# Narrower GpSimd pieces, another group order and fewer row transfers in a bidirectional mLSTM and attention encoder layer

## The chip, the cores and the metric

The kernel runs on one core of one Trainium2 chip. A core has a matrix engine (TensorE, PE in the profile, with PEld for its weight loads), a vector engine (VectorE, DVE), a scalar engine (ScalarE, ACT), GpSimd (POOL), a queue engine (SyncE, SP) that here only issues transfers, 16 DMA engines, the on-chip memory SBUF and the accumulator memory PSUM with 8 banks of 2 KB a partition. The metric is device time in microseconds of one execution, the median of several.

## What is computed

One encoder layer is applied with the same parameters to two sequences, of 256 and 1024 tokens (T = 1280 columns, NB = 10 blocks of 128), model width 1024. Cut to what matters here:

```python
h = rmsnorm(x, pre_mix_norm)
z = h @ w_in + b_in                       # all projections, float32 accuracy
ya = windowed_gqa_attention(aq, ak, av)   # 16 heads in 4 groups, window 128
ym = bidirectional_mlstm(mq, mk, mv, mo, mi, mf)   # 4 heads, both directions
merged = g_att * (ya @ w_att_branch) + g_mlstm * (ym @ w_mlstm_branch)
x = x + rmsnorm(merged @ w_out, post_mix_norm)
# then a gated FFN with a depthwise convolution, and a residual

# one chunk of 128 tokens of the mLSTM, one direction, one head (width 256)
a = (q @ k.T) * exp(d - m_t)              # masked decay weights
num = w_inter * (q @ C) + a @ v           # state product, values product
den = w_inter * (q @ n) + sum(a)
h = num / max(abs(den), exp(-m_t))
C_new = decay * C + wk.T @ v              # state, carried to the next chunk
```

## The kernel before, in words

**Units and groups.** Every weight matrix lies in HBM as units of 1024 x 128. A unit is loaded to `unit_raw` and split by GpSimd in `take` into a high part `unit_h` (a multiplication by one, rounded, line 701) and a low part `unit_l` (the rest, line 704). TensorE multiplies high by high, high by low and low by high, 8 inner tiles each, so one group (`unit_group`, lines 1762 to 1764) is 24 matmuls of 512 or, in each third group of a unit, 256 columns. For each of the 4 heads there are 22 groups M (mLSTM queries, keys, values and output gate; 12 and up run as `vo_group`, lines 1795 to 1797) and 21 groups A (gates, attention queries, keys, values). A group goes to PSUM bank 0 or 1; `group_tables` sets which, by the group's number modulo 2, and `bank_free` lets the group wait until the last user of its bank is copied out. There are five unit slots, so a load waits for the last group of the unit five before it.

**A head.** `mlstm(h)` runs 10 steps i. In step i the forward direction does chunk i and the backward one chunk 9 - i. On TensorE a step is: `m_numden` (state product of both directions, line 1856, and values product, line 1859, in banks 3 and 4), the forward state update (`m_update`, line 1873), the first A group that the table `A_STEP` names for the step, the backward update, scores and turned keys of the next step while i < 4 (`m_scores`, lines 1841 and 1843), and the other A groups of the step. A direction has no state product in its first chunk of a sequence. After the steps come the groups A18 to A20, then the first M group of the next head, and then `attend(h)`: ten blocks j, each with turned probabilities (line 1960), scores of the next block (line 1941), two M groups of the next head (`M_BESIDE`) and the values product (lines 1973 and 1974). The last head has no M groups to put beside its attention. After the four heads follow the branch, output and FFN products, which split their weights in another function, `split`.

**The other engines in a step.** VectorE, in its written order: `normalise_h(i)` (lines 1381 to 1396), forward `state` (line 1370 or 1372, c_st), `weights(i+1)` (line 1361, ex times the kept scores), from step 5 on `gated(i)` (lines 1407 and 1410), `gate_ahead(i+1)` (a reciprocal, line 1399), and then backward `state`. ScalarE makes the exponents `ex` from rows in `bw` (line 1049), copies scores and keys out of PSUM (`keep_scores`, lines 1056 and 1057), copies the groups out (line 978), and issues `load_rows` (line 1013), two transfers a step, one for each direction. GpSimd masks the rows (line 721), scales queries and keys (lines 730 and 745) and, after some steps (`A_TAKE`), takes a unit.

**Between heads.** `c_st`, the state, lies where `ya_st`, the attention's output, was staged. Before, VectorE ends `attend` with a wait for the transfers of `ya_st` to HBM (s_ya) and TensorE ends it with a wait for the last addition (a_o). The first thing that VectorE does in a head is to copy the head's columns (lines 1416 to 1421), for which ScalarE waits (m_sel) before its first exponents. The rows of steps 0 and 1 of the next head are loaded in attention block 9.

## Time and profile before

| | us |
|---|---|
| median of 3 runs (2757.56 to 2759.15) | 2758.14 |
| the profiled execution | 2762.94 |
| its span in the trace | 2761.1 |
| TensorE busy in it (92% of the span) | 2547.2 |
| VectorE busy | 1506.0 |
| GpSimd busy | 1170.9 |
| ScalarE busy | 665.6 |
| mean granted TensorE clock, as a share of full | 0.962 |

The profiled execution is 4.8 us above the median, and 1.8 us of it lie around the span. A busy share is an average over the whole program. The four heads take about the time from 170 to 1500 us of the trace; head 1 starts at 488, head 2 at 816, head 3 at 1143. TensorE's idle time is in few places, and each has a releaser, the instruction of another engine whose end let it go on.

### The profile page before, as it was taken

What the parts mean: (1) busy time and instruction counts of PE and PEld (TensorE: products, weight loads), DVE (VectorE), ACT (ScalarE), POOL (GpSimd) and SP (SyncE); (2) the same over time, 40 slices, a digit from 0 to 9 for tenths busy, and PEclk for the clock granted to TensorE, in tenths of its full rate; (3) what the DMA queues carried; (4) which work ended last, traced back from release to release, by engine and by line L of the source; (5) the groups of instructions that cost most, each with busy time, mean ns of one, the idle gap of its engine ahead of it and who ended that gap; (6) DMA issues with size and microseconds to landing.
All of it is one profiled execution on the core that took longest, in us unless ns stands there. A gap on an engine that the chain in (4) does not pass through costs nothing.

```text
span 2761.1 us, 37750 instructions
## 1 busy us (share of the span) xinstructions
PE 2547.2 (92%) x14636; PEld 2325.3 (84%) x14636; DVE 1506.0 (55%) x2133; ACT 665.6 (24%) x1511; POOL 1170.9 (42%) x658
## 2 busy tenths in 40 slices
PE   7999899898989899898688999897999999999996
PEld 4888778787878788786577899897999999999996
DVE  5524467154652647435674655888874217876312
ACT  4112333133422333223433112321110101110001
POOL 5434320342104421142412236565566656666663
PEclk9999999999999999999799999999999999999998
DMA  3122111331122211223234342323323343232321
GB/s 128 43 81 86 58 31 28 88 92 35 37 63 66 77 40 33 69 77 122 90 115 134 111 154 69 138 70 102 102 70 119 103 139 97 76 114 70 115 82 61
DMA packets 128583, 233.77 MB, mean 85 GB/s; under 512 B 11000, under 2 KB 73992, under 8 KB 128448
## 3 DMA queue, kind: packets, MB, share of 16 engines
q1 hardware_dynamic: 77920, 203.04, 22.6%
q10 hardware_dynamic: 50528, 28.89, 4.4%
q8 instruction: 89, 1.46, 0.2%
q14 instruction: 46, 0.38, 0.0%
HBM read 184.35 MB, written 47.46 MB: 84 GB/s over the span
## 4 chain that ended last, share of the span: by engine, by line
PE 79%; DVE 13%; ACT 3%; DMA 2%; DVEq 2%; issue 1%; SPq 0%; ACTq 0%
PE ps L1762 20%; PE ps L1764 20%; PE ps L1763 20%; PE ps L1795 2%; PE ps L1797 2%; PE ps L1941 2%; PE ps L1796 2%; PE ps L1960 2%; PE ps L1856 2%; PE ps L1873 2%; DVE prob L1470 2%; PE ps L1859 1%; DMA ya_scratch<-ya_st 1%; DVE acc L1605 1%; ACT prob L1143 1%
## 5 line engine op out<-in xcount | busy, mean ns | idle before, releaser
L690 POOL TENSOR_TENSOR ring_h<-raw,colt 128x1024 fp32r<-128x1024 f32 x168 | 326.7, 1945 | 649.4 <-PE ps L1764 645.0
L1762 PE MATMUL ps<-h_h,ring_h 128*128 128x320 f32 (+1 forms) x1408 | 439.9, 312 | 14.7 <-DVE f_z L1669 9.1
L1763 PE MATMUL ps<-h_l,ring_h 128*128 128x320 f32 (+1 forms) x1408 | 438.6, 312 | 0.0
L1764 PE MATMUL ps<-h_h,ring_l 128*128 128x320 f32 (+1 forms) x1408 | 438.5, 311 | 0.0
L693 POOL TENSOR_TENSOR ring_l<-raw,ring_h 128x1024 fp32r<-128x1024 f32 x168 | 415.8, 2475 | 23.9
L1762 PE MATMUL ps<-ht_h,unit_h 128*128 128x512 f32 (+1 forms) x1080 | 396.4, 367 | 5.9 <-ACT av_t L978 4.8
L1763 PE MATMUL ps<-ht_l,unit_h 128*128 128x512 f32 (+1 forms) x1080 | 383.9, 356 | 0.0
L1764 PE MATMUL ps<-ht_h,unit_l 128*128 128x512 f32 (+1 forms) x1080 | 383.9, 355 | 0.0
L1605 DVE TENSOR_TENSOR acc<-acc,sq 128x322 f32<-128x322 f32 (+1 forms) x84 | 114.9, 1368 | 311.9 <-ACT sq L816 310.1
L1762 PEld LDWEIGHTS ps<-h_h,ring_h 128*128 128x128 f32 x1408 | 267.3, 190 | 16.1 <-issue 9.8
L1764 PEld LDWEIGHTS ps<-h_h,ring_l 128*128 128x128 f32 x1408 | 267.6, 190 | 0.0
L1763 PEld LDWEIGHTS ps<-h_l,ring_h 128*128 128x128 f32 x1408 | 267.2, 190 | 0.4 <-issue 0.2
L701 POOL TENSOR_TENSOR unit_h<-unit_raw,colt 128x1024 fp32r<-128x1024 f32 x61 | 118.7, 1946 | 299.2 <-DMA unit_raw<-w 299.2
L1762 PEld LDWEIGHTS ps<-ht_h,unit_h 128*128 128x128 f32 x1080 | 205.7, 190 | 35.0 <-issue 6.4
L1764 PEld LDWEIGHTS ps<-ht_h,unit_l 128*128 128x128 f32 x1080 | 204.7, 190 | 29.4
L1763 PEld LDWEIGHTS ps<-ht_l,unit_h 128*128 128x128 f32 x1080 | 205.5, 190 | 27.9 <-issue 0.2
L721 POOL TENSOR_TENSOR bw<-bw,mask 128x256 f32<-128x256 f32 x40 | 29.3, 731 | 351.6 <-DMA bw<-rows_scratch 351.6
L1762 PE MATMUL ps<-ht_h,ring_h 128*128 128x512 f32 (+3 forms) x384 | 141.5, 368 | 19.0 <-DVE ht_l L1545 9.2
L704 POOL TENSOR_TENSOR unit_l<-unit_raw,unit_h 128x1024 fp32r<-128x1024 f32 x61 | 150.7, 2471 | 8.7
L1763 PE MATMUL ps<-ht_l,ring_h 128*128 128x512 f32 (+3 forms) x384 | 138.8, 362 | 0.0
L1764 PE MATMUL ps<-ht_h,ring_l 128*128 128x512 f32 (+3 forms) x384 | 138.6, 361 | 0.0
L1763 PE MATMUL ps<-f_z,ring_h 128*128 128x320 f32 x448 | 138.4, 309 | 0.0
(244 smaller groups left out, 5293.4 us busy)
## 6 DMA issues: line engine op xcount, KB each, us to landing
raw<-w SPq DMA_DIRECT2D x168, 512.0 KB, 3.6
unit_raw<-w SPq DMA_DIRECT2D x61, 512.0 KB, 3.9
bw<-rows_scratch ACTq DMA_DIRECT2D x80, 128.0 KB, 4.8
gate_scratch<-g_st SPq DMA_DIRECT2D x32, 256.0 KB, 3.9
xr<-xt SPq DMA_DIRECT2D x2, 2568.0 KB, 10.0
x_scratch<-x SPq DMA_DIRECT2D x2, 2568.0 KB, 8.9
zo_scratch<-o_st SPq DMA_DIRECT2D x40, 128.0 KB, 1.7
ym_scratch<-y_st ACTq DMA_DIRECT2D x40, 128.0 KB, 2.0
```

What stands on the lines that cost most here:

```text
L690: nc.gpsimd.tensor_tensor(ring_h[:, :, slot * P:(slot + 1) * P], raw[:, rslot], one_col.unsqueeze(2).to_broadcast([P, KT, P]), ALU.mult)
L693: nc.gpsimd.tensor_tensor(ring_l[:, :, slot * P:(slot + 1) * P], raw[:, rslot], ring_h[:, :, slot * P:(slot + 1) * P].bitcast(F32), ALU.su ...
L701: nc.gpsimd.tensor_tensor(unit_h[:, slot], unit_raw[:, slot], one_col.unsqueeze(2).to_broadcast([P, KT, P]), ALU.mult)
L704: nc.gpsimd.tensor_tensor(unit_l[:, slot], unit_raw[:, slot], unit_h[:, slot].bitcast(F32), ALU.subtract).then_inc(s_split, 1)
L1470: last = V.tensor_scalar(prob[:, r, a:b], prob[:, r, a:b], small[:, 36 + r:37 + r], None, ALU.mult)
L1605: V.tensor_tensor(acc[st][:, a:b], acc[st][:, a:b], sq[st][:, j % slots, 0:b - a], ALU.add)
L1762: mm(out_ap, wh, hi(k + k_first), start=first and k == 0, stop=False)
L1763: mm(out_ap, wh, lo(k + k_first), start=False, stop=False)
L1764: ins = mm(out_ap, wl, hi(k + k_first), start=False, stop=last and k == kts - 1)
L1795: mm(ps[:, g % 2, :], ht_h[:, k, t], unit_h[:, 0:4, k], start=k == 0, stop=False)
L1796: mm(ps[:, g % 2, :], ht_h[:, k, t], unit_l[:, 0:4, k], start=False, stop=False)
L1797: ins = mm(ps[:, g % 2, :], ht_l[:, k, t], unit_h[:, 0:4, k], start=False, stop=k == KT - 1)
```

## The change

Six edits. (1) `take` splits a unit in four pieces of two inner tiles (256 columns) for each of its two operations; `split` is left as it is. (2) In `m_numden` the values product is put in front of the state product; its wait (m_a) is now in front of those for the scaled queries (m_q) and the state (m_c). (3) Two A groups instead of one run ahead of step 0, and `A_STEP` shifts: step 0 has [2], step 3 only [7], step 8 has [16, 17], step 9 [18], and A19 and A20 come after; ScalarE's exponents of step 1 come ahead of the steps. (4) `load_rows` is one transfer a step for both directions, from a new scratch tensor in which the two rows of a chunk lie side by side (1 KB in a piece instead of 512 bytes); those of the next head are issued in attention block 8 instead of 9. (5) Banks alternate by a group's place in the whole order instead of its number. (6) For all but the last head, VectorE's wait for s_ya and TensorE's wait for a_o move from the end of `attend` into step 0 of the next head, to where the state and its bank are first written; for the last head VectorE's is left out, TensorE's stays.

The diff, its core:

```diff
-A_STEP = [[1]] + [[2 * i, 2 * i + 1] for i in range(1, 8)] + [[16], [17]]
+A_STEP = [[2], [3, 4], [5, 6], [7], [8, 9], [10, 11], [12, 13], [14, 15], [16, 17], [18]]
...
-        bank = key[2] % 2
+        bank = i % 2
...
+            for d in range(2):
+                sp.dma_start(uw_d.rearrange("(r c) q t -> r q c t", c=NB)[4 * d:4 * d + 4, 0],
+                             r_u[32 * d:32 * d + 4, :].rearrange("p (c t) -> p c t", t=P)).then_inc(p_out, 16)
...
-                nc.gpsimd.tensor_tensor(unit_h[:, slot], unit_raw[:, slot],
-                                        one_col.unsqueeze(2).to_broadcast([P, KT, P]), ALU.mult)
+                for k in range(0, KT, 2):
+                    nc.gpsimd.tensor_tensor(unit_h[:, slot, k:k + 2], unit_raw[:, slot, k:k + 2],
+                                            one_col.unsqueeze(2).to_broadcast([P, 2, P]), ALU.mult)
                 pool.drain()
-                nc.gpsimd.tensor_tensor(unit_l[:, slot], unit_raw[:, slot], unit_h[:, slot].bitcast(F32),
-                                        ALU.subtract).then_inc(s_split, 1)
+                for k in range(0, KT, 2):
+                    last = nc.gpsimd.tensor_tensor(unit_l[:, slot, k:k + 2], unit_raw[:, slot, k:k + 2],
+                                                   unit_h[:, slot, k:k + 2].bitcast(F32), ALU.subtract)
+                last.then_inc(s_split, 1)
...
-                pool.wait_ge(m_bw[i % 2], lin(lambda k: 32 * (5 * k + i // 2 + 1), h))
+                pool.wait_ge(m_bw[i % 2], lin(lambda k: 16 * (5 * k + i // 2 + 1), h))
...
-                for d in range(2):
-                    c = chunk_of(d, i)
-                    act.dma_start(bw[:, i % 2, d], rows_d[0:2, bass.ds(h + (4 * d + shift), 1), c * P:(c + 1) * P]
-                                  .rearrange("q o t -> o q t").to_broadcast([P, 2, P])).then_inc(m_bw[i % 2], 16)
+                a, b = [(4 * d + h + shift) * NB + chunk_of(d, i) for d in range(2)]
+                act.dma_start(bw[:, i % 2].rearrange("p d q t -> p d (q t)"),
+                              uw_d.rearrange("(o n) q t -> o n (q t)", o=1)[:, a:b + 1:b - a]
+                              .to_broadcast([P, 2, 2 * P])).then_inc(m_bw[i % 2], 16)
...
                 evac_a(0, h)
+                exponents(1, h)
+                evac_a(1, h)
                 for i in range(NB):
-                    if i + 1 < NB:
+                    if 1 <= i < NB - 1:
                         exponents(i + 1, h)
...
+                    if dense and j == NB - 2:
+                        act.wait_ge(a_s_done, lin(lambda k: NB * (k + 1), h))
+                        for i in range(2):
+                            load_rows(i, h, 1)
...
-                    if dense and j == NB - 1:
-                        act.wait_ge(a_s_done, lin(lambda k: NB * (k + 1), h))
-                        for i in range(2):
-                            load_rows(i, h, 1)
...
                 dve.wait_ge(m_cu[d], lin(lambda k: 8 * k + updates_to(d, i), h))
+                if i == 0 and h:
+                    dve.wait_ge(s_ya, 16 * NB * h)
...
-                dve.wait_ge(s_ya, lin(lambda k: 16 * NB * (k + 1), h))
...
                 else:
+                    pe.wait_ge(m_h, lin(lambda k: NB * k + i, h))
+                pe.wait_ge(m_a, lin(lambda k: NB * k + i + 1, h))
+                for d in range(2):
+                    ins = mm(ps[:, 3 + d, 0:DH + 1], ex[i % 2][:, side(d, i)], v_tok[:, chunk_of(d, i)],
+                             start=True, stop=fresh(d, i))
+                if i:
                     pe.wait_ge(m_q, lin(lambda k: 9 * k + i, h))
-                    pe.wait_ge(m_h, lin(lambda k: NB * k + i, h))
                 for d in range(2):
                     if not fresh(d, i):
                         pe.wait_ge(m_c[d], lin(lambda k: 8 * k + updates_to(d, i - 1), h))
                         for dt in range(2):
-                            mm(ps[:, 3 + d, 0:DH + 1], qw[:, d, dt], c_st[:, d, dt], start=dt == 0, stop=False)
-                pe.wait_ge(m_a, lin(lambda k: NB * k + i + 1, h))
-                for d in range(2):
-                    ins = mm(ps[:, 3 + d, 0:DH + 1], ex[i % 2][:, side(d, i)], v_tok[:, chunk_of(d, i)],
-                             start=fresh(d, i), stop=True)
+                            ins = mm(ps[:, 3 + d, 0:DH + 1], qw[:, d, dt], c_st[:, d, dt], start=False, stop=dt == 1)
                 ins.then_inc(m_nd, 1)
...
                 pe.wait_ge(m_wk, lin(lambda k: 9 * k + i + 1, h))
+                if i == 0 and d == 0 and h:
+                    pe.wait_ge(a_o, NB * h)
...
                 m_scores(0, h)
-                unit_group("A", 0, 0, h)
+                for g in range(2):
+                    unit_group("A", 0, g, h)
...
-                for g in range(18, 21):
+                for g in range(19, 21):
                     unit_group("A", g // 3, g % 3, h)
...
-                pe.wait_ge(a_o, lin(lambda k: NB * (k + 1), h))
+                    pe.wait_ge(a_o, NB * HEADS)
```

VectorE at the seam of heads 0 and 1, from the last addition of the attention to the first weights of the mLSTM. Before:

```order
L1517 TENSOR_TENSOR ya_st<-ya_st,ps 64x512 [waits a_out_lo_part]
L1416 COPY hc<-tokcol 128x10 [waits m_y_evacuated,ya_stored]
...
L1476 COPY hc<-colt 128x2
L1361 TENSOR_TENSOR ex_79<-ex_79,s_sv 128x256 [waits m_exp,m_scores_and_keys_kept]
L1381 SCALAR_TENSOR_TENSOR small<-ps,hc 128x2 [waits m_numden]
```

After:

```order
L1528 TENSOR_TENSOR ya_st<-ya_st,ps 64x512 [waits a_out_lo_part]
L1427 COPY hc<-tokcol 128x10 [waits m_y_evacuated]
...
L1487 COPY hc<-colt 128x2
L1370 TENSOR_TENSOR ex_79<-ex_79,s_sv 128x256 [waits m_exp,m_scores_and_keys_kept]
L1392 SCALAR_TENSOR_TENSOR small<-ps,hc 128x2 [waits m_numden]
...
L1381 COPY c_st<-ps 128x514 [waits ya_stored,m_update_fwd]
```

The wait for the stored attention output has moved from the copy of the columns to the first write of the state, which comes after the normalisation of step 0.

ScalarE at the same seam (bw are the rows, ex the exponents, s_sv and mk_t the kept scores and keys, g_st a group's copy). Before:

```order
L1151 ACTIVATE prob_h<-ps 128x512 x2
L1180 DMA ya_scratch<-ya_st 64x4x128
L1013 DMA bw<-rows_scratch 128x2x128 x4
L1175 ACTIVATE ya_st<-ps 64x512
L1180 DMA ya_scratch<-ya_st 64x4x128
L1049 ACTIVATE ex_79<-bw,tokcol 128x128 x2
L1056 ACTIVATE s_sv<-ps 128x256
L1057 ACTIVATE mk_t<-ps 128x2x2x128
L978 ACTIVATE g_st<-ps,hc 128x512
```

After:

```order
L1019 DMA bw<-exponent_rows_scratch 128x2x256 x2
L1184 ACTIVATE ya_st<-ps 64x512
L1160 ACTIVATE prob_h<-ps 128x512 x2
L1189 DMA ya_scratch<-ya_st 64x4x128
L1184 ACTIVATE ya_st<-ps 64x512
L1189 DMA ya_scratch<-ya_st 64x4x128
L1056 ACTIVATE ex_79<-bw,tokcol 128x128 x2
L1063 ACTIVATE s_sv<-ps 128x256
L1064 ACTIVATE mk_t<-ps 128x2x2x128
L985 ACTIVATE g_st<-ps,hc 128x512
```

Four row transfers in block 9 have become two in block 8, one block of the attention earlier.

TensorE at the end of step 0 of head 0 and the start of step 1 (a row of x2 stands for one direction's or both directions' matmuls). Before:

```order
L1873 MATMUL ps<-v_tok,wk 128x257 x2
L1841 MATMUL ps<-ident,mk_t 128x128 x2
L1843 MATMUL ps<-mq_t,mk_t 128x128 x2
L1841 MATMUL ps<-ident,mk_t 128x128 x2
L1843 MATMUL ps<-mq_t,mk_t 128x128 x2
L1856 MATMUL ps<-c_st,qw 128x257 x4
L1859 MATMUL ps<-v_tok,ex_80 128x257 x2
L1762 MATMUL ps<-ht_h,unit_h 128x256
```

After:

```order
L1852 MATMUL ps<-ident,mk_t 128x128 x2
L1854 MATMUL ps<-mq_t,mk_t 128x128 x2
L1852 MATMUL ps<-ident,mk_t 128x128 x2
L1854 MATMUL ps<-mq_t,mk_t 128x128 x2
L1864 MATMUL ps<-v_tok,ex_80 128x257 x2
L1872 MATMUL ps<-c_st,qw 128x257 x4
L1771 MATMUL ps<-ht_h,unit_h 128x512
```

Directly behind the scores stands now the values product, which needs the weights ex made from these scores. In step 4 the same rows follow one another after the change; before, the group A7 stood between the scores and step 4.

## Rows read from the trace of the kernel before

**Rows 1.** TensorE's waits from 187 to 1290: total us, times, longest.

```profile
PE ps L1856 <- DVE c_st L1370: 29.0, 7, 8.2
PE ps L1859 <- DVE ex L1361: 20.7, 3, 7.5
PE ps L1960 <- DVE prob L1470: 20.6, 9, 3.4
PE ps L1762 <- ACT av_t L978: 4.8, 3, 1.6
```

**Rows 2.** Timeline, seam of heads 0 and 1: start us, us, row, [idle before <-releaser].

```profile
487.30 4.51 SPq L481 DMA_DIRECT2D unit_raw<-w  x4
...
488.44 0.44 PE L1841 MATMUL ps<-ident,mk_t 128*128 128x128 f32 x2 [1.40 <-DVE ya_st L1517]
...
500.05 0.17 DVE L1416 COPY hc<-tokcol 128x10 f32<-128x10 f32 x1 [11.66 <-DMA ya_scratch<-ya_st]
...
502.95 2.05 PE L1859 MATMUL ps<-v_tok,ex 128*128 128x257 f32 x4 [7.49 <-DVE ex L1361]
```

**Rows 3.** Windows: us; busy PE, PEld, DVE, ACT, POOL; granted clock; DMA share, GB/s.

```profile
502.90:507.40 4.50, 4.45 (x11) 3.54 (x12) 2.00 (x6) 0.60 (x3) 4.36 (x4) 0.50 0.15 58
303.00:306.00 3.00, 3.00 (x7) 2.44 (x8) 0.00 (x0) 0.00 (x0) 0.00 (x0) 0.50 0.00 0
350.60:353.80 3.20, 3.14 (x15) 3.14 (x16) 0.00 (x1) 1.09 (x2) 0.00 (x0) 0.50 0.00 0
392.30:398.10 5.80, 5.72 (x25) 5.63 (x26) 0.62 (x2) 0.00 (x0) 0.00 (x0) 0.50 0.00 0
325.20:328.20 3.00, 3.00 (x13) 2.51 (x14) 0.00 (x0) 0.00 (x0) 0.96 (x1) 1.00 0.35 130
```

**Rows 4.** Timeline of head 0, steps 8 and 9.

```profile
286.40 0.16 DVE L1381 SCALAR_TENSOR_TENSOR small<-ps,hc 128x2 f32<-128x2 f32 x1 [3.56 <-PE ps L1859]
...
290.12 4.48 DVE L1407 TENSOR_TENSOR h_acc<-h_acc,o_ld_even 128x256 f32<-128x256 f32 x2
...
292.24 2.08 POOL L701 TENSOR_TENSOR unit_h<-unit_raw,colt 128x1024 fp32r<-128x1024 f32 x1
...
294.68 2.40 DVE L1410 SCALAR_TENSOR_TENSOR o_ld_even<-h_acc 128x256 f32<-128x256 f32 x1
...
302.99 2.08 PE L1856 MATMUL ps<-c_st,qw 128*128 128x257 f32 x4 [8.10 <-DVE c_st L1370]
```

**Rows 5.** Timelines of GpSimd and VectorE in the last head, steps 7 and 8.

```profile
1257.55 1.36 POOL L745 TENSOR_TENSOR wk<-mk_t,tokcol 128x256 f32<-128x256 f32 x2
...
1257.66 0.78 DVE L1361 TENSOR_TENSOR ex<-ex,s_sv 128x256 f32<-128x256 f32 x1
...
1269.55 0.76 DVE L1407 TENSOR_TENSOR h_acc<-h_acc,o_ld_even 128x256 f32<-128x256 f32 x2
```

**Rows 6.** GpSimd's line 745, all of it: duration ns min/median/max.

```profile
L745 POOL TENSOR_TENSOR wk<-mk_t,tokcol x64: 608/616/855, 173.8 to 1258.1; 128x256 f32<-128x256 f32 x64
```

**Rows 7.** The same for GpSimd's line 721.

```profile
L721 POOL TENSOR_TENSOR bw<-bw,mask x40: 723/732/743, 150.7 to 1265.9; 128x256 f32<-128x256 f32 x40
```

**Rows 8.** Timeline of head 0, the attention's blocks 0 and 1.

```profile
345.75 4.86 DVE L1470 TENSOR_SCALAR prob<-prob,small 128x256 f32<-128x256 f32 x4
...
350.66 1.97 PE L1960 MATMUL ps<-ident,prob 128*128 128x128 f32 x8 [3.43 <-DVE prob L1470]
...
392.38 1.97 PE L1960 MATMUL ps<-ident,prob 128*128 128x128 f32 x8 [3.11 <-DVE prob L1470]
```

**Rows 9.** Timeline of head 1, from the scores to the end of step 1's products.

```profile
514.66 1.03 PE L1856 MATMUL ps<-c_st,qw 128*128 128x257 f32 x4
...
515.76 0.43 DVE L1361 TENSOR_TENSOR ex<-ex,s_sv 128x256 f32<-128x256 f32 x1 [8.31 <-ACT mk_t L1057]
...
516.84 1.14 PE L1856 MATMUL ps<-c_st,qw 128*128 128x257 f32 x4 [1.15 <-DVE c_st L1370]
```

**Rows 10.** The page, sixth part: row transfers, KB each, us from issue to landing.

```profile
bw<-rows_scratch ACTq DMA_DIRECT2D x80, 128.0 KB, 4.8
```

More of the change, by code:

```diff
@@ L155, in build @@
     x1_d = nc.dram_tensor("x1_scratch", (2, KT, P, WIN), F32).ap()
-    rows_d = nc.dram_tensor("rows_scratch", (6, 8, T), F32).ap()
+    rows_d = nc.dram_tensor("rows_scratch", (4, 8, T), F32).ap()
+    uw_d = nc.dram_tensor("exponent_rows_scratch", (2 * HEADS * NB, 2, P), F32).ap()
     dec_d = nc.dram_tensor("decay_scratch", (8, NB), F32).ap()
@@ L531, in _ @@
             sp.wait_ge(p_args, 1)
-            for q, rows in ((0, r_u), (2, r_li), (3, r_f), (4, r_m), (5, r_b)):
+            for d in range(2):
+                sp.dma_start(uw_d.rearrange("(r c) q t -> r q c t", c=NB)[4 * d:4 * d + 4, 0],
+                             r_u[32 * d:32 * d + 4, :].rearrange("p (c t) -> p c t", t=P)).then_inc(p_out, 16)
+            for q, rows in ((0, r_li), (1, r_f), (2, r_m), (3, r_b)):
                 for d in range(2):
@@ L975, in evac @@
                 a, b = CHUNKS[key1[2] % 3]
-                src = ps[rows, key1[2] % 2, 0:b - a]
+                src = ps[rows, GROUPS[key1][1], 0:b - a]
                 act.wait_ge(d_done, lin(lambda k: GROUPS[key_of(k)][0] + 1, h))
@@ L1343, in evac_vo @@
                     dve.wait_ge(s_os[blk % 2], lin(lambda k: 16 * 5 * (k + shift), h))
-                bank = (12 + blk) % 2
+                bank = GROUPS[("M", h + shift, 12 + blk)][1]
                 V.tensor_tensor(v_tok[:, blk, 0:DH], ps[:, bank, 0:DH], bias_vo[:, 0:DH], ALU.add)
@@ L1777, in unit_group @@
                 g = 3 * u + c
+                bank = GROUPS[(kind, h + shift, g)][1]
                 unit = a_unit if kind == "A" else m_unit
@@ L1783, in unit_group @@
                 bank_free(pe, lambda k: (kind, k + shift, g), h)
-                dense(ps[:, g % 2, 0:b - a], in_unit(n1),
+                dense(ps[:, bank, 0:b - a], in_unit(n1),
                       (lambda k: ht_h[:, k, a:b], lambda k: ht_l[:, k, a:b]), before=before).then_inc(d_done, 1)
@@ L1792, in vo_group @@
                 bank_free(pe, lambda k: ("M", k + shift, g), h)
+                bank = GROUPS[("M", h + shift, g)][1]
                 t = slice(blk * P, (blk + 1) * P)
                 for k in range(KT):
-                    mm(ps[:, g % 2, :], ht_h[:, k, t], unit_h[:, 0:4, k], start=k == 0, stop=False)
-                    mm(ps[:, g % 2, :], ht_h[:, k, t], unit_l[:, 0:4, k], start=False, stop=False)
-                    ins = mm(ps[:, g % 2, :], ht_l[:, k, t], unit_h[:, 0:4, k], start=False, stop=k == KT - 1)
+                    mm(ps[:, bank, :], ht_h[:, k, t], unit_h[:, 0:4, k], start=k == 0, stop=False)
+                    mm(ps[:, bank, :], ht_h[:, k, t], unit_l[:, 0:4, k], start=False, stop=False)
+                    ins = mm(ps[:, bank, :], ht_l[:, k, t], unit_h[:, 0:4, k], start=False, stop=k == KT - 1)
                 ins.then_inc(d_done, 1)
@@ L1909, in mlstm @@
                         unit_group("A", g // 3, g % 3, h)
-                for g in range(18, 21):
+                for g in range(19, 21):
                     unit_group("A", g // 3, g % 3, h)
```

4 lines of the change are left out of this document (2 added, 2 removed).

## The prediction

> **What bounds the kernel now.** TensorE is busy for 92% of the span, so time comes or goes where it stands idle, or where it runs at half clock. I read first its list of waits from 187 to 1290 us, which is the four heads without the last attention [rows 1]: 29.0 us for the state (7 times: three of about 8.1 and four of 1.15), 20.7 for the first weights of a head (3 times), 20.6 for the normalised probabilities (6 of 3.1 to 3.4, the rest below 0.6), 4.8 for the copy of A20. Then I went to each place in the timeline. At the seam of two heads TensorE waits 1.40 us for the attention's last addition and, one group later, 7.49 us for the weights; VectorE stood 11.66 us until the attention's output had landed, and everything in the new head hangs on it [rows 2]. In step 9 of head 0 TensorE waits 8.10 us for the backward state while VectorE's operations on two SBUF operands take over 2 us each [rows 4]; in the last head, where GpSimd takes no unit there, two of them take 0.76 together and there is no such wait [rows 5]. In attention blocks 0 and 1 four multiplications of VectorE take 4.86 us beside a unit's split, and TensorE waits 3.43 and 3.11 [rows 8]. Last, the clock: behind each wait of over 3 us TensorE works at 1.2 GHz (granted 0.50) for 3.0 to 5.8 us; behind the 1.6 us wait for A20's copy it keeps 2.4 GHz (1.00) [rows 3]. A long wait therefore costs its length and about half of the slow stretch behind it.
>
> **The seams (edits 3, 4 and 6).** Removed: 20.7 us for the weights [rows 1] and 3 x 1.40 = 4.2 for the addition [rows 2], together 24.9. Behind each, 4.5 us at half clock [rows 3] cost 2.2, at three seams about 6.4. In the new order VectorE copies the columns right after the last addition at 488.4; columns, exponents, copied keys and weights took 502.8 - 500.0 = 2.8 us [rows 2], so the weights are ready at about 491.5. TensorE has the scores (488.44 to the next group, an estimate of 1.3 from 8 small products) and now two groups ahead of step 0. A matmul of 512 columns takes 3.00 / 13 = 0.23 us [rows 3], a group of 24 thus 5.5, one of 256 columns about half, 2.9. Step 0 is reached at about 487 + 1.3 + 11 = 499, with 8 us in hand. What is late next? The moved wait of VectorE stands in front of the first state, due at about 501.6 (step 0's product and the normalisation behind it); the output landed before 500.05 [rows 2], and queued behind that wait are only the weights and state of step 1, not due before 506. TensorE's moved wait is 11 us late. The row masks are made on GpSimd before the seam, as the transfers leave one block (some 9 us or more) earlier. So I take the full gain, **31.3 us**. If the output lands 3 us later nothing changes; from some 5 us on it would.
>
> **State of step 9 (edits 1, 2 and 3).** From the end of step 8's products (286.40) to the state is 302.99 - 286.40 = 16.6 us on VectorE, of which TensorE waits 8.1 and fills 8.5 [rows 4]. The new order puts group A17 (2.9) and the values product (0.9) into the stretch: 12.3 filled. VectorE's chain: two operations of line 1407 took 4.48 where 0.76 is their time [rows 4, 5], so one loses 1.9; with the two of line 1410 (2.40 for the first, which is of the same size) and the weights, 1.0, five operations lose some 8.4 us. When GpSimd works in pieces of 256 columns, an operation can lose at most one piece: 0.61 for the first kind (line 745 has that size and a multiplier that is spread the same way) [rows 6], 0.73 for the second [rows 7], so 5 x 0.65 = 3.3. The chain becomes 16.6 - 5.1 = 11.5, below 12.3: no wait. Three times 8.1 is 24.4, and 1.5 for each slow stretch [rows 3] adds 4.5: **28.9 us**. Without any help from the pieces 16.6 - 12.3 = 4.3 would stay.
>
> First what the row shows: a VectorE operation on two SBUF operands lasts 2 us beside a long GpSimd instruction, 0.4 without [rows 4, 5], and in the last head one of 0.78 got in between two GpSimd instructions of line 745, since it ended at 1258.44 and they at 1258.91 [rows 5]. The Trainium skill, SBUF — State Buffer, section Who interferes with whom, says that the pair of ports shared by the two engines is an exclusive lock, held for the whole instruction by whichever issued first. By that rule read strictly, four pieces already queued on GpSimd would be served before VectorE, and the edit would do nothing (rival 3); the last head's row speaks for taking turns.
>
> **Attention blocks 0 and 1 (edit 1).** Here four multiplications follow one another, each loses a piece: 345.75 + 4 x (0.57 + 0.27) = 349.1 instead of 350.6, if the pieces are back to back. I take 1.5 us for block 0 and 1.4 for block 1, three heads: 8.7 of 18.9. The waits that stay (1.9 and 1.7) lie between the 1.6 us behind which the clock stayed and the 3.1 behind which it fell; of the half clock's 1.6 + 2.9 = 4.5 us a head [rows 3] I take 1, so 3 in all. Together **11.7**; bounds 0 and 18.9 + 13.5 = 32.4.
>
> **Banks (edit 5).** M0 follows A20 in the other bank, the wait of 3 x 1.6 us goes [rows 1]: **4.8**. The copy of A20 is now due only in front of M0's last inner tile, 21 of 24 matmuls or 4.8 us later, which is three times what TensorE waited for it.
>
> **Costs.** (a) Values in front: in step 1 TensorE started the forward state product during the wait; ex was ready at 516.19, 1.5 us after the scores, and the state at 516.8 [rows 9]. Now the values start at 516.2 and three products of 0.9 (four matmuls, 1.03 with the pipeline's end [rows 9]) follow, ending at 518.9, where the old order ended at 518.6: 0.3 x 4 = 1.2. (b) Step 3 loses its second group, so step 4's values stand right behind the scores: a new wait of 1.5, four heads, 6.0. Together **-7.2**. (c) A take of 8 pieces is, by starts 0.04 closer than the durations of [rows 6, 7], 4 x 0.57 + 4 x 0.69 and a drain of 0.14, 5.2 us; its long first operation alone took 1.9 to 2.1 [rows 4], so the whole grows by some 0.8. Queued behind it is the scaling of the queries, which TensorE needs; at the tightest place, step 5, the transfer, the mask, the take and the scaling need 4.8 + 0.7 + 5.3 + 1.5 = 12.3 us [rows 7, 10] of the 16 that the step's products give. Nothing, and it could cost 0 to 1 us. (d) One transfer with larger pieces instead of two: between 0 and 0.5 us of ScalarE's issue time gained, off the path.
>
> **Sum.** 31.3 + 28.9 + 11.7 + 4.8 - 7.2 = 69.5 us. The profiled execution, 2762.9, would be 2693.4. It stands 4.8 above the median, and I set the difference against the median: 2758.1 - 69.5 = 2688.6, **2688**. A measurement of this kernel tells about 0.2% (5.5 us) from no change.
>
> **Rivals.** 1. The pieces free VectorE wholly (it gets the port at once): blocks 0 and 1 give 32.4 instead of 11.7, 2668. For it: the normal duration of the four is only 1.1 to 1.4 us; against: two GpSimd pieces are back to back in [rows 5]. 2. The new waits of steps 1 and 4 (some 1.5 us each) tip the clock as the longer ones do: 8 x 1.6 = 12.8, 2701. The 1.6 us wait that kept the clock [rows 3] speaks against, but it had full groups on both sides. 3. VectorE waits for all queued pieces: block gain 0, in step 9 4.3 us and 1.5 of slow clock stay, 3 times: -11.7 - 17.4, 2717. 4. At the seam a new wait takes half: the four unit loads queued at 487.30 [rows 2] stand ahead of the store of gate group 0 in SyncE's queue, and its buffer is now wanted by group A2 some 6 us sooner after them; a store landing 5 us late costs 5 us at each seam: 2703. 5. **Slower**: the row transfer in its new form lands late. It stands ahead of mask, take and query scaling; the slack at the tightest step is 16 - 12.3 = 3.7 us over the 4.8 of now [rows 10]. Beyond a landing of 8.5 us each us is lost in the 20 steps with a take, so from 12 us on the 69.5 are eaten and the kernel is slower; at 13 us it gives 2688 + 20 x 4.5 = 2778. The bytes are the same and the pieces larger, so little speaks for it.
>
> **Chances.** Forecast 0.48, rival 1 0.15, rival 2 0.14, rival 3 0.08, rival 4 0.10, slower 0.02, and 0.03 for cases that meet near no change. The range 2666 to 2712 takes in the forecast and rivals 1, 2 and 4 (0.87, less some for their own spread). Faster 0.95, same 0.02, slower 0.03.
>
> **What would show it.** Right: in the new trace no wait of TensorE over 1 us at the seams and at step 9; the 8 us waits gone from the waits list with their half-clock stretches; VectorE's longest operation on lines of gated and the multiplications near 1.1 us instead of 2.4; new waits of about 1.5 us for the weights in steps 1 and 4, eight in all; waits of about 1.8 in blocks 0 and 1. Wrong: VectorE operations still above 2 us there (rival 3), a granted 0.50 behind steps 1 and 4 (rival 2), ScalarE waiting for a gate store in step 0 (rival 4), or row transfers over 8 us (rival 5).

## The result and the profile after

| kernel | median us (lowest to highest, runs) | ratio to the kernel before, 95% interval |
|---|---|---|
| before | 2757.85 (2756.75 to 2759.15, 4) | |
| changed | 2677.54 (2674.70 to 2683.36, 4) | 0.9711, 0.9693 to 0.9729 |

The change makes the kernel 80.3 us faster; the prediction said 69.5, and its range (2666 to 2712) holds the time. The profiled execution of the changed kernel took 2683.4 us, span 2681.6.

First TensorE's list of waits in the changed kernel, from 187 to 1290 us (instruction and its line, what it waited for, then total us, times, longest), to be held against [rows 1]. The program is 80 us ahead by then, so this stretch now takes in the last head's attention, to which all lines but the `ex` one and part of the first belong (its waits, 7.7, 7.5, 5.0 and 9.2, stand in the trace of before too, later):

```profile
PE ps L1975 <- DVE prob L1481: 21.2, 11, 7.7
PE ps L1864 <- DVE ex L1370: 12.1, 8, 1.5
PE ps L1771 <- DVE ht_l L1556: 9.2, 1, 9.2
PE ps L1956 <- DVE q_st_first L1511: 7.5, 1, 7.5
PE ps L1988 <- DVE prob_l L1522: 5.5, 2, 5.0
PE ps L1906 <- ACT av_t L985: 1.6, 1, 1.6
```

The 29.0 us for `c_st` and the 20.7 for the first weights are gone. What is new is 12.1 us for `ex`, in eight waits of 1.5: the two predicted for each head, in steps 1 and 4. Of the first line 10.3 us lie in the attention of heads 0 to 2 (20.6 before). The one wait of 1.6 for `av_t` is that of the last head.

The seam of heads 0 and 1, timeline of the changed kernel (start us, us, row, [idle before <-releaser]), answering [rows 2]:

```profile
471.72 0.38 PE L1852 MATMUL ps<-ident,mk_t 128*128 128x128 f32 x2
...
472.54 0.68 DVE L1528 TENSOR_TENSOR ya_st<-ya_st,ps 64x512 f32<-64x512 f32 x1 [0.79 <-ACT ya_st L1184]
...
473.31 0.17 DVE L1427 COPY hc<-tokcol 128x10 f32<-128x10 f32 x1
...
475.66 0.43 DVE L1370 TENSOR_TENSOR ex<-ex,s_sv 128x256 f32<-128x256 f32 x1 [1.69 <-ACT mk_t L1064]
...
483.97 1.03 PE L1864 MATMUL ps<-v_tok,ex 128*128 128x257 f32 x4
```

The scores start without a wait. VectorE copies the columns right behind the last addition, and the weights are ready at 476.1, 7.9 us before TensorE wants them. The output, issued at 473.25, landed after 4.4 us here and after 8.0 and 8.3 at the other two seams (11.5, 11.2 and 9.9 before).

Steps 8 and 9 of head 0, timeline of the changed kernel, answering [rows 4]:

```profile
290.71 0.16 DVE L1392 SCALAR_TENSOR_TENSOR small<-ps,hc 128x2 f32<-128x2 f32 x1 [3.82 <-PE ps L1872]
...
292.15 2.70 POOL L706 TENSOR_TENSOR unit_h<-unit_raw,colt 128x256 fp32r<-128x256 f32 x4
...
293.72 1.42 DVE L1418 TENSOR_TENSOR h_acc<-h_acc,o_ld_even 128x256 f32<-128x256 f32 x2
...
295.22 0.80 DVE L1421 SCALAR_TENSOR_TENSOR o_ld_even<-h_acc 128x256 f32<-128x256 f32 x1
...
295.95 0.94 DVE L1421 SCALAR_TENSOR_TENSOR o_ld_even<-h_acc 128x256 f32<-128x256 f32 x1
...
300.09 0.62 DVE L1381 COPY c_st<-ps 128x514 f32<-128x514 f32 x1
...
301.04 1.03 PE L1864 MATMUL ps<-v_tok,ex 128*128 128x257 f32 x4
```

Beside GpSimd's four pieces the pair of line 1418 takes 1.42 us (4.48 before) and one of line 1421 0.80 to 0.94 (2.40 before). From `small` to the end of the state's copy are 10.0 us (16.6 before), and the copy ends 0.3 us before TensorE starts on step 9.

Attention blocks 0 and 1 of head 0, timeline of the changed kernel, answering [rows 8]:

```profile
338.35 2.63 DVE L1481 TENSOR_SCALAR prob<-prob,small 128x256 f32<-128x256 f32 x4
...
341.04 1.09 PE L1975 MATMUL ps<-ident,prob 128*128 128x128 f32 x8 [1.21 <-DVE prob L1481]
...
379.94 1.09 PE L1975 MATMUL ps<-ident,prob 128*128 128x128 f32 x8 [1.84 <-DVE prob L1481]
```

Last the windows of the clock in the changed kernel (us; busy PE, PEld, DVE, ACT, POOL; granted clock; DMA share, GB/s), answering [rows 3]: behind the new waits of steps 1 and 4, and behind the wait of block 1 in heads 0, 1 and 2.

```profile
193.60:197.60 4.00, 3.99 (x18) 3.45 (x19) 1.35 (x5) 0.69 (x2) 3.56 (x7) 1.00 0.31 125
235.40:239.40 4.00, 3.99 (x20) 3.56 (x21) 1.41 (x5) 1.94 (x4) 3.87 (x7) 1.00 0.21 57
379.94:383.36 3.42, 3.42 (x26) 3.34 (x27) 0.68 (x2) 0.22 (x1) 1.22 (x2) 1.00 0.00 0
679.96:683.38 3.42, 3.42 (x16) 3.23 (x16) 0.28 (x1) 0.34 (x1) 0.00 (x0) 0.50 0.00 0
978.37:981.79 3.42, 3.42 (x26) 3.33 (x27) 0.70 (x2) 0.24 (x1) 1.22 (x2) 1.00 0.02 5
```

Only one stretch at 1.2 GHz is left between 187 us and the last head's attention: 3.42 us behind the 1.84 us wait of head 1, worth 1.7 us. The same wait of 1.84 us in heads 0 and 2 left the clock at 2.4 GHz.

By stage, from the starts of a head's first scores and of the attention's first transposes (line 1906 of the changed kernel, 1892 of the one before) in the two traces (us):

| stage | before | changed | difference | forecast |
|---|---|---|---|---|
| start to head 0 | 170.6 | 172.9 | +2.3 | 0 |
| heads 0 to 3 up to the attention | 160.3, 170.2, 170.5, 152.6 | 150.5, 150.6, 150.5, 146.7 | -55.3 | -53.6 |
| attention of heads 0 to 2 | 157.6, 157.1, 157.2 | 148.3, 149.7, 147.2 | -26.7 | -15.9 |
| from there to the end | 1465.2 | 1465.0 | -0.2 | 0 |

(The forecast's 31.3 for the seams is split here: the 4.2 us for the last addition lie in the attention's rows.) The part that went better than forecast is the attention.

### The profile page after: what moved, and what is told of

Same layout as the page of the kernel before. It is cut to its first block, busy times and chain, and to the rows that moved or that the text cites. A ratio compares the mean times of both kernels' runs of the same rounds, so it can differ in the third digit from the quotient of the medians.

```text
span 2681.6 us, 38115 instructions
## 1 busy us (share of the span) xinstructions
PE 2522.5 (94%) x14636; PEld 2308.7 (86%) x14636; DVE 1471.3 (55%) x2133; ACT 664.6 (25%) x1511; POOL 1240.2 (46%) x1024
## 4 chain that ended last, share of the span: by engine, by line
PE 83%; DVE 11%; ACT 2%; DVEq 2%; issue 1%; DMA 1%; ACTq 0%; SPq 0%
PE ps L1771 21%; PE ps L1772 21%; PE ps L1773 21%; PE ps L1806 3%; PE ps L1808 3%; PE ps L1807 3%; PE ps L1956 2%; PE ps L1872 2%; PE ps L1887 2%; PE ps L1975 2%; DVE prob L1481 1%; PE ps L1864 1%; DVE acc L1614 1%; ACT prob L1152 1%; DVE small L1459 1%
## 5 line engine op out<-in xcount | busy, mean ns | idle before, releaser
L1771 PE MATMUL ps<-h_h,ring_h 128*128 128x320 f32 (+1 forms) x1408 | 441.1, 313 | 17.4 <-DVE f_z L1678 11.5
L706 POOL TENSOR_TENSOR unit_h<-unit_raw,colt 128x256 fp32r<-128x256 f32 x244 | 155.7, 668 | 197.9 <-DMA unit_raw<-w 197.9
L710 POOL TENSOR_TENSOR unit_l<-unit_raw,unit_h 128x256 fp32r<-128x256 f32 x244 | 186.8, 797 | 8.7
L1773 PE MATMUL ps<-f_z,ring_l 128*128 128x320 f32 x448 | 138.4, 309 | 0.0
```

The costliest lines, as they stand in the source:

```text
L706: nc.gpsimd.tensor_tensor(unit_h[:, slot, k:k + 2], unit_raw[:, slot, k:k + 2], one_col.unsqueeze(2).to_broadcast([P, 2, P]), ALU.mult)
L710: last = nc.gpsimd.tensor_tensor(unit_l[:, slot, k:k + 2], unit_raw[:, slot, k:k + 2], unit_h[:, slot, k:k + 2].bitcast(F32), ALU.subtract)
L1771: mm(out_ap, wh, hi(k + k_first), start=first and k == 0, stop=False)
L1773: ins = mm(out_ap, wl, hi(k + k_first), start=False, stop=last and k == kts - 1)
```

## Experiments

Two runs put a single edit into the kernel before; the others alter the changed kernel in what is named with each. Line numbers differ by a few between the kernels. The kernel before took 2758.1 to 2758.8 us (medians) beside them.

**Wide pieces again.** Edit 1 undone, all else as changed.

```
-                for k in range(0, KT, 2):
-                    nc.gpsimd.tensor_tensor(unit_h[:, slot, k:k + 2], ...
+                nc.gpsimd.tensor_tensor(unit_h[:, slot], unit_raw[:, slot],
+                                        one_col.unsqueeze(2).to_broadcast([P, KT, P]), ALU.mult)
```

> The changed kernel with the unit split undone: each of the two operations over 1024 columns again, all else as changed. Theory (VectorE loses one GpSimd instruction per operation on two SBUF operands, so width sets the loss): in step 9 the chain is 16.6 us against 12.3 of cover, a wait of some 4.3 us returns in heads 0 to 2; the waits of attention blocks 0 and 1 go from 1.2 and 1.8 back to about 3.4 and 3.1, and the half clock behind all of them returns (1.5, 1.6 and 2.9 us); in all 3 x (4.3 + 1.5 + 2.2 + 1.3 + 4.5) = 41 us more, about 2719. Rival (the attention's gain came from the new group order and the bank alternation, and step 9 is covered by the moved group alone): 5 us or less more, 2683.

Measured: 2721.7 us, ratio 0.9865 (0.9848 to 0.9881). Timeline of this kernel, head 0, step 9:

```profile
294.91 2.08 POOL L705 TENSOR_TENSOR unit_h<-unit_raw,colt 128x1024 fp32r<-128x1024 f32 x1
...
295.16 2.11 DVE L1415 TENSOR_TENSOR h_acc<-h_acc,o_ld_even 128x256 f32<-128x256 f32 x1
...
297.35 2.46 DVE L1418 SCALAR_TENSOR_TENSOR o_ld_even<-h_acc 128x256 f32<-128x256 f32 x1
...
305.72 1.81 PE L1869 MATMUL ps<-c_st,qw 128*128 128x257 f32 x4 [4.42 <-DVE c_st L1378]
```

Each of VectorE's operations again lasts until 0.3 us behind the end of the GpSimd instruction beside it. TensorE waits 4.4 us in step 9 of three heads (4.3 was forecast for this case) and 3.0 to 3.4 in blocks 0 and 1, and the granted clock falls to 0.50 at all nine. The other edits do not bring this gain; the pieces do: 44.2 us.

**Pieces alone.** The kernel before with edit 1 and nothing else.

> The kernel before with one edit, GpSimd's pieces of 256 columns. Theory: the chain of step 9 shrinks from 16.6 to about 10.5 us, against 8.5 of cover, so the wait falls from 8.1 to about 2 us, three times 6 and the half clock of 1.5; blocks 0 and 1 gain 2.5 + 1.3 and 4.5 of half clock each head; 3 x 15.8 = 47, about 2710. The seam waits of 7.5 us and the 1.6 us wait for the copy of A20 stay. Rival (pieces matter only together with the moved group): under 15 us less than before.

Measured: 2712.9 us, ratio 0.9837 (0.9821 to 0.9853), 45.9 us faster than the kernel before beside it. TensorE's waits in this kernel, 187 to 1290 us:

```profile
PE ps L1963 <- DVE prob L1473: 21.3, 11, 8.1
PE ps L1862 <- DVE ex L1364: 19.7, 3, 7.8
PE ps L1859 <- DVE c_st L1373: 10.2, 7, 2.4
```

Of 24.4 us at step 9 (three waits of 8.1) 5.5 stay (1.57, 1.57, 2.40), and block 1 waits 1.84 us in each head, with the clock at 1.00 behind it; the seams keep 19.7 (20.7 before) and 3 x 1.40. So from both sides the pieces are worth 44 to 46 us, more than half of the whole.

**The moved waits alone.** The kernel before with edit 6 and nothing else.

```
+                if i == 0 and h:
+                    dve.wait_ge(s_ya, 16 * NB * h)
-                dve.wait_ge(s_ya, lin(lambda k: 16 * NB * (k + 1), h))
```

> The kernel before with edit 6 alone: VectorE's wait for the landed attention output and TensorE's wait for the last addition moved into step 0 of the next head; one group ahead, rows in block 9 by four transfers, long pieces. Theory: the moved waits alone give the whole of the seams, 3 x (1.4 + 6.9 + 2.1) = 31 us, since scores and one group (6.8 us) cover the 3 us that columns, exponents and weights take: about 2727. Limit: the first rows' mask was ready only 0.9 us after the last addition, so little is in hand. Rival (the rows in block 9 or the single group hold the seam open): a wait of 2 us or more for the weights stays at each seam, 2735 or more.

Measured: 2733.2 us, ratio 0.9918 (0.9901 to 0.9934), 25.3 us faster, where 31 were expected. The waits for `ex` and for the last addition are gone, but 4.2 us come back in another place (2.32, 1.18 and some 0.7), which the expectation had not named. Waits of TensorE, 187 to 1290 us, and the timeline at the start of head 2, in this kernel:

```profile
PE ps L1875 <- POOL wk L745: 4.2, 3, 2.3
```

```profile
814.50 0.72 POOL L721 TENSOR_TENSOR bw<-bw,mask 128x256 f32<-128x256 f32 x1 [4.30 <-DMA bw<-rows_scratch]
...
815.18 1.18 POOL L745 TENSOR_TENSOR wk<-mk_t,tokcol 128x256 f32<-128x256 f32 x2
...
816.41 1.51 PE L1875 MATMUL ps<-v_tok,wk 128*128 128x257 f32 x4 [2.32 <-POOL wk L745]
```

GpSimd waited for the last of the four row transfers (issued 5.0 us before the output's, landed after 11.7), with the scaled keys behind it in its order. The row transfers of the next head were the next thing to be late. The run with one group ahead of step 0, further down, has as little cover there and no such wait; it differs in edits 1, 2, 4 and 5 and most of edit 3, of which only edit 4 touches these transfers. No run undoes edit 4 beside edit 6, so that it is edit 4 is argued and not shown.

**The moved waits undone.** The changed kernel without edit 6.

> The changed kernel with edit 6 undone: VectorE again waits at the end of the attention for the landing of its output, TensorE for the last addition. Theory: the weights are ready at about 502.8 on head 1's old clock; TensorE has scores and two groups, 12.3 us, from 488.4, so it waits 1.4 + 2 us at each of three seams, and the clock may fall once or more: 10 to 17 us more, 2688 to 2695. Rival (the two groups ahead do nothing for the seam): the whole 31 us, 2708.

Measured: 2683.1 us, ratio 0.9733 (0.9717 to 0.9749), 5.5 us slower than the changed kernel by the medians; the intervals overlap, the profile shows 4.2 us of waits. Timeline of this kernel at the seam of heads 0 and 1:

```profile
471.96 0.44 PE L1852 MATMUL ps<-ident,mk_t 128*128 128x128 f32 x2 [1.40 <-DVE ya_st L1526]
...
480.25 0.17 DVE L1425 COPY hc<-tokcol 128x10 f32<-128x10 f32 x1 [8.35 <-DMA ya_scratch<-ya_st]
...
482.59 0.42 DVE L1370 TENSOR_TENSOR ex<-ex,s_sv 128x256 f32<-128x256 f32 x1 [1.68 <-ACT mk_t L1064]
...
484.27 1.03 PE L1864 MATMUL ps<-v_tok,ex 128*128 128x257 f32 x4
```

My expectation of 2 us of waiting for the weights failed: only the 1.40 came back, three times. VectorE waits 8.35 us for the output to land, 11.66 before the change [rows 2]. With two groups ahead of step 0 TensorE arrives at 484.27, 1.3 us after the weights. Why the output lands 3 us sooner was then open: the transfers of the rows are fewer, earlier and in larger pieces.

**Two row transfers in block 9, in 1 KB pieces; then in 512 byte pieces.** Both leave edit 6 undone, so that the landing shows in VectorE's wait. The first puts the row transfers back in number and place, with 1 KB source pieces; the second differs from it only in where the two rows of a step lie in the scratch tensor, so that a piece is 512 bytes again.

```
-    uw_d = nc.dram_tensor("exponent_rows_scratch", (2 * HEADS * NB, 2, P), F32).ap()
+    uw_d = nc.dram_tensor("exponent_rows_scratch", (2, 2 * HEADS * NB, P), F32).ap()
```

> The changed kernel with edit 6 undone and the row transfers again two a step and, for the next head, in block 9 (pieces stay 1 KB). In the run with edit 6 alone undone the output landed 7.3 to 8.5 us after its issue, against 9.9 to 11.5 in the kernel before, and TensorE waited only 1.4 us a seam. Theory (the four row transfers of block 9 stood in the way of the output's transfer): the output lands 10 to 11.5 us after its issue again, the weights come 13 to 14.5 us after the last addition against 12.3 of cover, a wait of 1 to 2.5 us returns: 3 to 8 us more than that run, 2686 to 2691. Rival (the landing got faster for another reason): landing as there, below 8.6 us, and no wait beyond 1.4.

> The changed kernel with the wait for the attention's output back at the end of each head (edit 6 undone), two row transfers a step, issued in block 9, as before, and the source rows again 512 bytes long each (the two exponent rows lie apart). It differs from the run that took 2680.2 us in the length of the source pieces alone, 512 bytes for 1 KB; there the row transfers landed 3.4 to 4.6 us after their issue, the last output transfer of a head 7.1 to 8.4 us after its own, and PE did not wait for weights. Theory: the short pieces are what held up the transfers behind them before the change (rows 5.1 to 11.6 us, output 9.9 to 11.5 us). Then the rows land after 5 to 11 us, the output after 9.5 to 11.5 us, PE waits 1 to 3 us a head for GpSimd's products or VectorE's exponentials behind it, and the time is 2684 to 2692. Rival: the position or the order of groups did it; then the output lands within 8.6 us, no wait returns and the time is 2680 within 3 us.

Measured: 2680.2 us (0.9713, 0.9696 to 0.9729) with 1 KB pieces, 2682.9 us (0.9725, 0.9709 to 0.9741) with 512 bytes; these times overlap in their runs, the landings do not. Sixth part of the profile's page (KB each, median us from issue to landing), first of the 1 KB kernel, then of the 512 byte one:

```profile
bw<-exponent_rows_scratch ACTq DMA_DIRECT2D x80, 128.0 KB, 3.3
```

```profile
bw<-exponent_rows_scratch ACTq DMA_DIRECT2D x80, 128.0 KB, 5.0
```

The last output transfer of a head landed 8.3, 7.0 and 8.4 us after its issue with 1 KB pieces and 9.3, 9.6 and 11.2 us with 512 bytes (before the change 11.5, 11.2 and 9.9). Timelines of the seam, first 1 KB (heads 1 and 2), then 512 bytes (heads 2 and 3):

```profile
779.07 0.17 DVE L1424 COPY hc<-tokcol 128x10 f32<-128x10 f32 x1 [7.17 <-DMA ya_scratch<-ya_st]
...
784.26 1.03 PE L1863 MATMUL ps<-v_tok,ex 128*128 128x257 f32 x4
```

```profile
1083.70 0.17 DVE L1424 COPY hc<-tokcol 128x10 f32<-128x10 f32 x1 [11.28 <-DMA ya_scratch<-ya_st]
...
1086.61 1.10 PE L1863 MATMUL ps<-v_tok,ex 128*128 128x257 f32 x4 [1.67 <-DVE ex L1369]
```

The first expectation (10 to 11.5 us again with 1 KB pieces) failed: the number and place of the transfers change nothing (7.9 us in the mean, 8.0 with the two transfers of block 8). The length of their pieces does. Over all profiles read, the last output of a head landed after 7.0 to 8.5 us behind row transfers in 1 KB pieces with edit 6 undone (six seams of two kernels), and after 9.3 to 11.5 us behind 512 byte ones (twelve seams: this run, the kernel before, and it with edit 1 or edit 6 alone). Of the four row transfers of block 9 the last landed within 4.6 us in 1 KB pieces, before the output was issued, and after 10.0 to 10.5 us in 512 byte ones, some 5 us behind the output's issue. In means, 2.1 of the 2.9 us come back with the short pieces; the other 0.8 stay open, and single seams differ by more than that between kernels with the same transfers. With a landing of 11.2 us the wait for the weights is back (1.67); with 9.6 it is not. Before the change a landing of this size cost 7.5 us, since one group less stood in front of step 0. The edits cover one another here: with edit 6 undone, or edits 4 and 6, most of the seam's gain stays, and so it does without the second group of edit 3 (next run).

**One group ahead of step 0.** Edit 3 taken back by one group: one group ahead, step 0 has one, steps 1 to 8 two, step 9 one.

```
-A_STEP = [[2], [3, 4], [5, 6], [7], [8, 9], [10, 11], [12, 13], [14, 15], [16, 17], [18]]
+A_STEP = [[1]] + [[2 * i, 2 * i + 1] for i in range(1, 9)] + [[18]]
```

> The changed kernel with one group instead of two ahead of step 0, and the table [1], [2, 3] to [16, 17], [18]: step 3 has two groups again, so scores and products of step 4 are apart. Theory: with edit 6 the weights are ready 3 us after the attention's last addition, and scores and one group, 6.8 us, cover that; VectorE's wait for the landed output lasts longer into step 0 but nothing of step 0 needs it before the scores of step 1; so no wait at the seams, and the four waits of 1.5 us in step 4 go: 6 us less than the changed kernel, about 2671. Rival (the second group is what covers the landing of the output): 3 to 5 us more at each seam, 2686 to 2692.

Measured: 2669.65 us, ratio 0.9682 (0.9666 to 0.9698), 7.9 us faster than the changed kernel. The line for `ex` in its waits, 187 to 1290 us:

```profile
PE ps L1862 <- DVE ex L1368: 6.1, 4, 1.5
```

Four of the eight waits of 1.5 are gone, as expected (6.0 us). At the seams no wait appears: a second group ahead buys nothing once edit 6 is there.

**A full first step.** The same, but the steps are filled 2, 2, 2, 2, 2, 2, 2, 1, 2, 1, so that steps 0 to 3, in which the scores of the next step are made, have two groups each, and the first short one is step 7.

```
+A_STEP = [[2 * i + 1, 2 * i + 2] for i in range(7)] + [[15], [16, 17], [18]]
```

> The changed kernel with one group ahead of step 0 and the table [1, 2], [3, 4] to [13, 14], then [15], [16, 17], [18]: every step with scores of the next one has a group behind the scores, and the single group stands in step 7, after which no backward state is due. Theory: the remaining four waits of 1.5 us for the weights of step 1 go as well; nothing new appears, since from step 7 to 8 only the forward state and the weights are needed, both ready within 4 us: 6 us below the run with one group ahead, 2664. Rival (step 7, shorter by 5.5 us, makes VectorE or GpSimd late: gate, masks, exponents): waits of 1 us or more in step 8, 2670 or above.

Measured: 2661.6 us, ratio 0.9649 (0.9633 to 0.9665), 15.9 us faster than the changed kernel. No line for `ex` is left in its list of waits, as expected.

**Pieces of 128 columns**, first in the changed kernel, then on top of the last one.

> The changed kernel with 8 pieces of 128 columns for each operation of the unit split. Theory (an operation of VectorE loses at most one GpSimd instruction): a piece is about 0.35 to 0.4 us, so the waits of attention block 0 (0.5 to 1.2 us) shrink to near nothing and those of block 1 (1.84) to about 1; a take grows from 5.2 to some 6 us. TensorE's waits there in all 3 to 4 us less. Rival (the fixed part of the shorter instructions eats it, or the remaining wait of block 1 is not from the contention): block 1 keeps 1.8.

> The changed kernel with one group ahead of step 0, the steps filled in the order 2,2,2,2,2,2,2,1,2,1 groups, and the pieces of GpSimd's split cut from 256 to 128 columns. The kernel with that order of groups and 256 column pieces took 2661.6 us; its waits for VectorE's exponentials in the dense heads' attention blocks were 0.95, 0.79 and 0.74 us in block 0 and 1.40, 1.71 and 1.84 us in block 1. The changed kernel with 128 column pieces alone had no wait in block 0 and 0.86, 0.98, 0.98 us in block 1. If the two add up, the waits fall by 2.5 + 2.1 = 4.6 us and the time is 2657, 2654 to 2660. Rival: the units come late, since splitting one takes GpSimd 7.2 us (8 x 0.42 + 8 x 0.48) instead of 5.5 us and this order asks for groups earlier; then new waits for a split stand at the heads of units and the time is 2662 or more.

Measured: 2673.4 us for the first (one run), with no wait in block 0 and 0.86, 0.98, 0.98 in block 1, as expected. For the second 2661.5 us, ratio 0.9647 (0.9631 to 0.9663): nothing on top. In the attention its heads take 146.9, 146.4 and 145.8 us for 148.0, 147.5 and 147.5, a gain of 3.9, but head 0 starts at 176.7 us instead of 174.0. TensorE's waits in its first 187 us:

```profile
PE ps L1804 <- POOL unit_l L710: 5.0, 1, 5.0
```

In the kernel with 256 column pieces this line is not there. Ahead of head 0 GpSimd has a row of units to split, and eight pieces twice over cost it more per unit (means from 187 to 1290 us: 0.42 and 0.48 us a piece of 128, 0.63 and 0.76 of 256, so 7.2 us a unit for 5.6), so one unit comes 5 us late. (GpSimd is busy for 39.6 of the 40 us from 60 to 100 us there; with 128 columns in the changed kernel alone TensorE waits 2.4 and 1.5 us for it ahead of head 0.) It is the rival of the expectation, at a place that I had not named.

**Banks by the group's number again** (edit 5 undone), and **the state product in front again** (edit 2 undone).

```
-        bank = i % 2
+        bank = key[2] % 2
```

> The changed kernel with the banks given by the number of the group again, not by its place in the order (edit 5 undone). Prediction's term: the wait of 1.61 us for ScalarE's copy out of the bank comes back behind each dense head's last A group (three places, 4.8 us); with a stretch at half clock behind each it could be up to 4 us more. Expected 2682.5, 2681 to 2687. Rival: the bank is free by then, since the last groups stand elsewhere in the order now; then the time is 2677.5 within 2 us.

> The changed kernel with the state product in front of the values product again in each step (edit 2 undone). In the profile of the changed kernel the copy of the state in step 9 ended at 300.71 us and the values product began at 301.04: with the order turned round the state is there 0.3 us before it is wanted, so step 9 should stay without a wait. In steps 1 and 4 the waiting goes over from the exponentials (ready at 193.47) to the copy of the state behind them on VectorE (194.1): waits 0.3 to 0.7 us longer, less the values product that then runs behind instead of ahead. Expected: 2677 to 2682, that is, edit 2 by itself is worth 0 to 4 us. Rival: the state's copy is late in step 9 in other heads, by 0.5 to 1.5 us each, and the clock falls behind it; then 2684 or more.

Measured: 2680.9 us (0.9719, 0.9703 to 0.9735) and 2676.1 us (0.9700, 0.9683 to 0.9718). Waits of TensorE, 187 to 1290 us, first with the banks, then with the products turned round:

```profile
PE ps L1771 <- ACT av_t L985: 4.8, 3, 1.6
```

```profile
PE ps L1868 <- DVE c_st L1383: 4.8, 4, 1.2
PE ps L1868 <- DVE c_st L1381: 4.6, 4, 1.2
```

The banks are worth their three waits (4.8 us in the profile; the 3.4 between the medians is within the intervals). Turning the products round is worth nothing that these runs can tell: eight waits of 1.2 for the state take the place of eight of 1.5 for the weights, and step 9 has no wait either way. They are 0.3 us shorter each, where I had expected them longer: with the state in front TensorE has done its first product before it waits for the second state (the wait lies between two instructions of line 1868). That is the 0.3 x 4 of cost (a) of the prediction, and the profile gives it for all eight.

## Why the prediction was right, and where it was off

The time lies in the range, and the course was right; of the 10 us that the kernel did better than forecast, nearly all come from one term.

**The seams**, forecast 31.3. Right in size and in course: no wait over 1 us, the weights 2.9 us behind the last addition (forecast 3.1) and 8 us in hand, as forecast. The heads' part before the attention gained 55.3 us where this term, step 9, the banks and the costs together said 53.6. What the prediction had not seen is how the parts share it. Edit 6 alone brings 25.3 us in the kernel before, and edit 6 undone costs 5.5 in the changed one. Nor had it seen that the output would land sooner; it allowed only for a later landing.

**Step 9**, forecast 28.9. Right: no wait, no half clock. The chain was forecast at 11.5 us and measured at 10.0: an operation loses at most one piece, as forecast (the five lose about 1.8 us, 0.4 each, not 3.3; what one loses is less than a whole piece where it comes in the middle of one). "Without any help from the pieces 4.3 would stay" came out at 4.4. By the Trainium skill, SBUF — State Buffer, section Who interferes with whom, the shared port pair is an exclusive lock, and whoever issues first has it for the whole instruction. (The page says the latter of VectorE's modes that use both ports; of an instruction with two SBUF inputs it says that it contends with GpSimd's reads.) The rows agree with a lock that lasts an instruction (2.11 us beside a GpSimd instruction of 2.08 with wide pieces). They do not agree with reading it as a queue, in which all waiting pieces go first (rival 3, 2717): VectorE gets its turn after one piece.

**Attention blocks 0 and 1**, forecast 11.7. This is the term that was mis-sized. Its stage gave 26.7, of which 4.2 belong to the seam: 22.5. The waits were nearly right: 18.9 us before, 8.1 left (1.21, 0.86, 0.46 and three of 1.84), so 10.9 gained where 8.7 was forecast. The rest, 22.5 - 10.9 = 11.6, is the clock, for which I had taken 3. The half clock behind these waits cost 4.5 us a head before [rows 3], 13.5 in all, and the changed kernel keeps 1.7 of it; that the difference is 11.8 bears the 11.6 out. The step that was off is the share of the clock that the shortened waits would give back, taken as 1 us of 4.5 a head because they lie between the 1.6 us behind which the clock stayed and the 3.1 behind which it fell: of the three waits of 1.84, the only ones in that gap, two did not lower the clock, and the three shorter ones did not either. Rival 1 counted the whole of the clock, 13.5, but with no waits left at all.

**Banks**, forecast 4.8: the profile shows it with the edit undone, 4.8.

**Costs**, forecast -7.2. Eight new waits of 1.51 us, as named; the run with one group ahead, in which the four of step 4 are gone, is 7.9 us faster (6.0 was the forecast's figure for them). The clock stayed at 1.00 behind all eight, so rival 2 fell. Rival 4: ScalarE's waits at the three seams name no store. Rival 5: the new row transfer lands in 3.6 us (median; 4.8 at the most), not late. The take showed no cost in heads 0 to 3 with 256 columns; with 128 it showed 5 us at the start.

**Sum.** 10.8 from the attention, 1.7 from the heads, 0.2 at the end, less 2.3 at the start, make the 10 us between the forecast of 69.5 and the 79.5 between the two spans. The 2.3 at the start lie in the first norms (waits of 18.3 us there for 15.7) and the clock, and may be no effect of the change: over the profiles of all kernels with pieces of 256 columns head 0 starts between 170.8 and 175.3 us, and with wide ones between 170.6 and 173.1.

## What to carry to other kernels

Where VectorE's operations stand on the path and the trace shows them stretched to the length of the GpSimd instruction beside them, cut that instruction: here four pieces for one took 44 to 46 us off, while the other five edits together brought some 36. A reordering that opens a new wait for every one that it closes has to be counted wait by wait: of the six edits here one bought nothing that the runs can tell and half of another cost 8 us, and with the short step moved to where no wait hangs on it (step 7) the kernel took 2661.6 us, less than both. And shortening a wait can be worth more than its length: the waits of block 1 went from 3.1 to 1.84 us, and in two heads of three the half clock behind them went too.

## What the runs showed of the hardware

- **The clock behind a wait.** In the profiles of the changed kernel and of eight others TensorE has the same wait of 1.84 us in block 1 of a head 22 times; behind 20 of them the granted clock stayed at 1.00, behind two it fell to 0.50 (in the changed kernel from 679.96 to 683.38, beginning 1.5 us after the wait's end; ahead of it lay 38 us without a wait over 1 us, as in the heads where the clock stayed). Up to the last attention it stayed behind all waits of 1.5 to 1.7 us (77 of them in fourteen profiles), and fell at one of 2.32, one of 2.40 and all of 3.0 and more. That two equal waits can differ, at 1.7 us a time, may be part of the spread between executions of one kernel (2674.7 to 2683.4); this was not tested.
- **Short pieces in a transfer.** 128 KB in pieces of 512 bytes landed in 5.0 us (median), in pieces of 1 KB in 3.3. An output transfer issued 5.4 us behind the last of them landed 1 to 2.8 us later with the short ones; the last of these was then still under way. I had taken the larger pieces for worth up to 0.5 us of ScalarE's issue time and nothing else.
- **Turns between VectorE and GpSimd.** An operation of VectorE on two SBUF operands that alone takes 0.42 us took 0.7 to 0.95 beside pieces of 0.6 to 0.8 us, 2.1 to 2.5 beside instructions of 2.1 to 2.4, and never waited for two GpSimd instructions in the rows read. The attention's multiplications, which have one SBUF operand and a scalar, are stretched too: four took 2.63 us beside pieces and 4.86 beside wide instructions.
